# V rows of the expert mix in one transfer for four expert tiles

## What is computed

```
def block(hb):                                # hb: 128 tokens x 1024
    q = (hb @ wq).reshape(n, 8, 2, 128)
    s = einsum('thpk,hpnk->thpn', q, keys)
    ...                                       # top 16 of 128 x 128 key pairs per head
    eidx, gw = chosen experts (8 heads x 16), softmax of their scores
    a = einsum('thkd,td->thk', u_tab[eidx], hb)
    w = gelu(a) * gw
    return einsum('thk,thkd->td', w, v_tab[eidx])
```

## Time and profile before

| | |
|---|---|
| runs | 5314.53, 5320.29, 5320.93 us; median 5320.29 |
| profiled execution | span 5317.0 us; its total time beside the span is not given |
| VectorE busy | 3482.5 us, 65% |
| TensorE busy | 4329.9 us, 81% |
| second stage of the mixer, layer 0 | from 2088.7 to about 2956 us |
| second stage of the mixer, layer 1 | from 4664.5 to about 5282 us |
| V loads (line 1907) | 256 transfers of 512 KB |
| activation loads (line 1906) | 128 of 192 KB, 128 of 128 KB |
| gathers of V (line 1917) | 640 |
| gate loads (line 1905) | 8 of 3 MB, 8 of 2 MB |

### The profile page before, as it was taken

One profiled execution on the slowest core, in us unless ns is written; L12 is line 12 of the kernel. 1 busy time (PEld: TensorE's weight loads), 2 busy tenths in 40 slices (PEclk: granted clock), 3 DMA queues, 4 the chain that ended last, 5 costly groups with the idle time before them and its releaser, 6 DMA issues. The chain is left out here.

```text
span 5317.0 us, 58819 instructions
## 1 busy us (share of the span) xinstructions
PE 4329.9 (81%) x21260; PEld 3195.8 (60%) x21260; DVE 3482.5 (65%) x6809; ACT 1481.4 (28%) x2724; POOL 1522.0 (29%) x1488
## 2 busy tenths in 40 slices
PE   6976788889999994887888676677689998867886
PEld 5854786766666663444445434333468888756776
DVE  3146763249979786787788534899329968645665
ACT  2125322223445553000000224544223455500000
POOL 0000330004324454344444000355003334333441
PEclk8988898989999996899899878888889999988987
DMA  4211002139879999999999100111238989999996
GB/s 160 64 65 64 5 5 80 48 146 352 317 273 340 414 404 394 363 394 392 378 383 393 50 18 9 42 48 44 79 120 321 342 334 398 376 364 402 403 403 240
DMA packets 465036, 1252.92 MB, mean 236 GB/s; under 512 B 52055, under 2 KB 186957, under 8 KB 459117
## 3 DMA queue, kind: packets, MB, share of 16 engines
q0 software_dynamic: 184320, 671.17, 32.9%
q1 hardware_dynamic: 275984, 569.51, 29.0%
q10 hardware_dynamic: 4444, 8.48, 0.4%
HBM read 1146.24 MB, written 102.76 MB: 235 GB/s over the span
## 5 line engine op out<-in xcount | busy, mean ns | idle before, releaser
L1935 PE MATMUL banks<-acts_in,v_rows 128*128 128x384 f32 (+1 forms) x4096 | 1161.2, 446 | 304.5 <-DMA v_rows<-peer_v 173.3
L1558 PE MATMUL banks<-h_dense,u_t 128*128 128x384 f32 (+1 forms) x4096 | 1205.8, 438 | 0.0
L1935 PEld LDWEIGHTS banks<-acts_in,v_rows 128*128 128x128 f32 x4096 | 796.3, 196 | 669.1 <-DMA v_rows<-peer_v 194.4
L1532 POOL DMA_INDIRECT rows<-peer_u,expert x640 | 633.5, 990 | 1508.6 <-DVE weight L1835 816.2
L1558 PEld LDWEIGHTS banks<-h_dense,u_t 128*128 128x128 f32 x4096 | 750.7, 193 | 249.1 <-issue 4.4
L1835 DVE CUSTOM_DVE_ANT_0 rows<-rows,banks 128x1024 f32<-128x1024 f32 x640 | 764.9, 1211 | 197.7 <-DMA rows<-peer_u,expert 132.5
L1917 POOL DMA_INDIRECT v_fetched<-peer_v,expert x640 | 608.1, 950 | 862.1 <-DVE banks L1997 745.0
L1997 DVE SCALAR_TENSOR_TENSOR banks<-v_fetched,weight,banks 128x1024 f32<-128x1024 f32 x630 | 783.3, 1279 | 0.0
L1926 ACT COPY y_tok<-banks 128x1024 f32<-128x1024 f32 x5 | 5.1, 1012 | 1461.7 <-DVE banks L1997 1461.7
L1973 DVE TENSOR_TENSOR acts_in<-acts_in,gates 128x384 f32<-128x384 f32 (+1 forms) x256 | 124.6, 487 | 431.1 <-DMA acts_in<-activations 431.0
L1617 ACT COPY u_t<-banks 128x512 f32<-128x512 f32 x512 | 300.2, 587 | 300.8 <-PE banks L1549 298.3
(11 more groups left out here) (403 smaller groups left out, 6239.0 us busy)
## 6 DMA issues: line engine op xcount, KB each, us to landing
u_raw<-peer_u SPq DMA_DIRECT2D x256, 512.0 KB, 7.9
v_rows<-peer_v SPq DMA_DIRECT2D x256, 512.0 KB, 15.2
gate_table<-part SPq DMA_DIRECT2D x20, 2048.0 KB, 11.8
activations<-acts SPq DMA_DIRECT2D x128, 192.0 KB
gates<-gate_table SPq DMA_DIRECT2D x8, 3072.0 KB, 22.8
acts_in<-activations SPq DMA_DIRECT2D x128, 192.0 KB, 12.4
peer_wq_in<-peer_wq SPq DMA_DIRECT2D x16, 1024.0 KB, 5.4
ada_ring<-ada_w SPq DMA_DIRECT2D x32, 512.0 KB, 3.9
```

The costliest lines, as they stand in the source:

```text
L1532: pool.indirect_dma_start(out=ring[:, s % U_RING, :], out_offset=None, in_=rows_of_u, in_offset=bass.IndirectOffsetOnAxis(ap=expert[:, t, ...
L1558: last = nc.tensor.matmul(out, u_t[:, i % 2, k * P:(k + 1) * P], h[:, k], start=(k == 0), stop=(k == DK - 1))
L1935: return nc.tensor.matmul(y_at(m if RESIDENT else j // GROUP * DK + m), v[:, j % V_ROWS, m * P:(m + 1) * P], acts[:, j % V_ROWS], start=st ...
```

## The change

Instead of one load of 512 KB for each expert tile, the first tile of a group issues one load of 2 MB for the group's four tiles. The order of issue in a group becomes: gates where due, activations of tile 0, V of tiles 0 to 3, activations of tiles 1, 2 and 3. The semaphores of V are two instead of eight, one for each half of the ring, and TensorE's `ready(j)` waits for the half in which j lies.

```diff
@@ -1869,7 +1869,7 @@
-        v_loaded, acts_loaded = ([a.sem(f"{name}{r}") for r in range(V_ROWS)] for name in ("v_loaded", "acts_loaded"))
+        v_loaded, acts_loaded = ([a.sem(f"{name}{r}") for r in range(n)] for name, n in (("v_loaded", V_ROWS // GROUP), ("acts_loaded", V_ROWS)))
@@ -1904,7 +1904,9 @@
                 sp.dma_start(acts[:, j % V_ROWS], acts_d[j]).then_inc(acts_loaded[j % V_ROWS], 16)
-                sp.dma_start(v[:, j % V_ROWS:j % V_ROWS + 1], v_rows[:, j:j + 1, :]).then_inc(v_loaded[j % V_ROWS], 16)
+                if r == 0:
+                    sp.dma_start(v[:, j % V_ROWS:j % V_ROWS + GROUP], v_rows[:, j:j + GROUP, :])\
+                        .then_inc(v_loaded[i % (V_ROWS // GROUP)], 16)
                 if j == V_ROWS - 1:
                     sp.dma_start(g.x_t[:], x_d).then_inc(x_loaded, 16)
@@ -1928,7 +1930,7 @@
             def ready(j):
-                pe.wait_ge(v_loaded[j % V_ROWS], 16 * (j // V_ROWS + 1))
+                pe.wait_ge(v_loaded[j % V_ROWS // GROUP], 16 * (j // V_ROWS + 1))
                 pe.wait_ge(weighted, j + 1)
```

## The result

The changed kernel takes 5349.66 us (median of 4 runs, 5341.98 to 5354.22) against 5320.61 for the kernel before (4 runs). The ratio is 1.0054, 95% interval 1.0039 to 1.0068: slower by 29 us. That is on the side that was forecast and inside the range, and about twice the predicted 15 us. The profiled execution has a span of 5346.0 us against 5317.0, which is the same 29 us.

What follows compares the result with a forecast made beforehand. Layer 0 was taken as bound by VectorE's work plus activation waits, layer 1 by nearly full DMA and TensorE. Terms 63 - 38 - 6 - 2 - 2 gave +15 us, predicted 5335 us, range 5296 to 5366.

Steps and rivals of the forecast that it cites:

- the distance of 7.5 to 8 us: Sign in layer 0: a group's first and second multiplies that far apart, with a wait near 2.75 us.
- TensorE's group-wide semaphore: V's semaphore standing for a whole group: nothing in layer 0; in layer 1 counted in that layer's -2 us.
- The wait before the second multiply: Layer 0, mid-block: V delays the second activation tile, a new VectorE wait of 2.75 us in 23 groups, +63 us.
- What comes back at the gates: Layer 0: fewer gathers under way shorten each of seven gate waits by 5.5 us, -38 us.
- First multiplies: Layer 0, activation waits outside gates and startup: TensorE catches up, SP issues earlier, -6 us (0 to -12).
- The second multiply behind gates: Layer 0, behind a gate load: q0 has run dry, so the wait there is only 0.2 us.
- Issues: SP in each layer: 96 fewer issues of 0.43 us; SP mostly waits for TensorE anyway, so nothing.
- Layer 1: Lower DMA floor against TensorE needing all four V tiles behind gates: -2 us, bounds -10 and +8.
- TensorE's chain of 72.9 us: Layer 1, per block: 59.6 us of products plus a 13.3 us gap, which does not get shorter.
- the DMA's floor: Layer 1: larger packets save 12 us of DMA time, lowering the floor by 1.5 us a block.
- the DMA is the bound, bigger packets simply pay: Rival for the whole kernel: gate waits absorb the new wait, engine time saved gives -22, 5298 us; chance 0.22.
- The fixed cost per transfer: Rule of 2.0 us per DMA plus bytes, about 4936 us; rival of a fixed queue cost, 5301 us, chance 0.01.

Runs made afterwards that it cites:

- e1: The changed kernel with the 2 MB load of V behind the group's four activation tiles instead of behind the first; ratio to the kernel before 0.9989.
- e2: The kernel before with its four 512 KB loads of V moved up behind the group's first activation tile; ratio to the kernel before 1.0285.
- e6: The changed kernel with V in transfers of two tiles (1 MB, 8 KB to a partition) and four semaphores; ratio to the kernel before 0.9971.
- e4: The change made in layer 1 alone, layer 0 as in the kernel before; ratio to the kernel before 0.9971.
- e3: The kernel before with its four 512 KB loads of V moved down behind the group's four activation tiles; ratio to the kernel before 1.0000.
- e7: The kernel before with each gate load but the first issued behind the loads of the group before; ratio to the kernel before 1.0002.
- e9: The kernel before with each gate load cut in four, the quarters issued behind the loads of the four groups before; ratio to the kernel before 0.9944.

## Why the prediction was right

**Who waits, and for what.** That layer 0 is VectorE's fixed work plus its waits for activations held: waits +39.8 us, time +42 us, work unchanged. Of the signs that the prediction named, the distance of 7.5 to 8 us (8.0) and the 64 transfers came as said; the gate waits are 14.1 us and not 12, the waits in layer 0 222.8 and not near 200, and layer 1's block, 71.7 us, is just under its 72 to 75. That TensorE's group-wide semaphore costs layer 0 nothing held too: e1 has it and has no loss.

**The wait before the second multiply** was the main term, computed as 2.75 us and 63 us from a packet of 16 KB at the rate of x's packets and turns of one each. Measured: 2.87 us in the mean and 66.0 us, the single waits 2.0 to 4.7 us. e2 and e6 put two other numbers to the same rule, 7.1 and 0.4 us expected, 6.3 and 0.4 measured. The page counts 64 transfers of V of 2048 KB and 248336 packets in q1 in place of 275984. That is 27648 fewer: 24576 where four V packets of 4 KB became one of 16 KB, and 3072 more, which is 16 for each of the 192 transfers fewer.

**What comes back at the gates** is the term that failed: -38 forecast, -22 measured, 16 of the 23 us by which layer 0's +17 fell short of +39.8. Its mechanism was right. The gathers issued about a gate load (from 6 us before it to 1 us after) land fast in the changed kernel, here for the load at 2536.82:

```profile
DMA to landing us min/median/max: 5.2/5.3/5.6
```

Over the seven loads the medians are 5.1 to 7.0 us, so few gathers are backed up there any more, and the gate loads themselves land 2.9 us sooner in the median. The seven of layer 0, before and after:

```profile
DMA to landing us min/median/max: 21.3/22.9/23.8
...
DMA to landing us min/median/max: 17.3/20.0/21.0
```

Two steps of the size were off. I took the 13.5 us of one block as the state of all: over the seven loads before the change the medians are 10.0 to 13.7 us, 12.1 in the mean against 5.9 after, so (12.1 - 5.9) / 1.7 = 3.7 gathers or 4.8 us were to be had on the average, not 6.2. And in the first 4 us after the issue of a gate load its own packets hardly come, while q0 runs on. The queues in those 4 us, before (from 2507.47) and after (from 2536.82):

```profile
q0 software_dynamic: 430, 1.57, 98.3%
q1 hardware_dynamic: 36, 0.06, 4.1%
```

```profile
q0 software_dynamic: 302, 1.08, 78.2%
q1 hardware_dynamic: 89, 0.18, 12.1%
```

Before the change 128 gather packets more went out of the way before the gates came, 8 for each engine or 1.3 us (over the seven loads q0 moved 439 packets in the mean before and 306 after). On this account they never cost the gate load anything. 4.8 - 1.3 is 3.5 us; measured are 22.0 / 7 = 3.1. The sum fits; no run tests this second step by itself.

**First multiplies** gave 3.7 of the 6 us. **The second multiply behind gates** has the 0.2 us that I computed and then left out of the sum, but 1.8 us behind the first of the loads, 3.2 us together.

**Issues** were put at nothing because eight take under 4 us. That holds in mid-block and not behind gates: in layer 0 before the change one issue of 7.1 to 9.3 us follows each of the seven gate loads, and several of the next ones take about 1.8 us and not 0.43. From SyncE's timeline, behind a gate load and in the next group:

```profile
2405.81 8.25 SPq L1906 DMA_DIRECT2D acts_in<-activations  x1
2414.10 2.46 SPq L1907 DMA_DIRECT2D v_rows<-peer_v  x1
...
2445.33 0.43 SPq L1907 DMA_DIRECT2D v_rows<-peer_v  x1
```

The changed kernel has such issues too, so nothing was gained or lost by it that these runs show.

**Layer 1** was forecast at -2 and gave -14. The step that failed is TensorE's chain of 72.9 us, which I said would not get shorter. TensorE's busy time in the six blocks is 58.6 us a block before and 58.2 after; I had put 59.6, 16 times the 3.72 us of one tile's row. And the one gap of 13.3 us behind the gates was not all its waiting. TensorE's waits for V (its weight loads) in one block, in us, times and longest, before and after:

```profile
PEld banks L1935 <- DMA v_rows<-peer_v: 17.1, 5, 13.7
...
PEld banks L1937 <- DMA v_rows<-peer_v: 14.6, 2, 14.3
```

The gap behind the gates grew by 0.6 us, as the prediction had feared, but the small waits for V in the middle of the block went. Over layer 1 TensorE's waits for V fell from 131.2 us to 121.4 and its busy time from 472.0 to 467.9, which together are the 14 us:

```profile
L1937 PE MATMUL banks<-acts_in,v_rows 128*128 128x256 f32 x2048 | 467.9, 393 | 121.4 <-DMA v_rows<-peer_v 121.4
```

What stays is the DMA's floor, which I had at -1.5 us a block and which is measured as -1.4 (73.1 to 71.7). The startup and the first block gave the rest, about 6 us. So the rival "the DMA is the bound, bigger packets simply pay" is true of layer 1, and e4 has it alone. Windows of layer 1 from 4800 to 5200 us bear it out: 402 to 403 GB/s in every kernel with 4 KB packets there (before, e2, e3, e7, e9), 406 in e6 with 8 KB, 407 to 408 in every one with 16 KB. It is false of layer 0, where the changed kernel leaves the DMA at 369 GB/s.

**The fixed cost per transfer.** With 192 transfers fewer the time rose, and the 4936 us of the single rule weighed in the prediction are 414 us away. The fit that it rests on stands in the Trainium skill, "DMA: Bandwidth & Descriptors", not in the section on bandwidth but under "Anatomy of one DMA — SWDGE (gpsimd) path", for transfers that GpSimd issues; V's loads are issued by SyncE and stand in a queue that is kept full, and no run here shows that cost.

**Clock.** The six blocks of layer 0 have a mean granted clock of 0.93 of 2.4 GHz after and 0.92 before, so these rows show no loss of clock by the new short waits, as assumed.

The two misses, 16 us at the gates and 12 us in layer 1, have opposite signs. Layer 0 by itself was forecast at +17 and came out at +42; that the total was only 14 us off is in part luck.

## What to carry to other kernels

When small transfers are merged, the order of the queue changes with them: a small load that stands behind the merged one is late by the time that the merged one takes, and here that decided more than the number of transfers. Compute where the next consumer's tile lands against when it asks, and put the small tiles that an engine needs soon ahead of the large one that it needs late. The same holds for a rare large load in front of frequent small ones: with the gate loads cut in pieces and spread over the groups, the gate waits in layer 0 fell from 121.0 to 5.3 us and the layer took 34 us less, where issuing them earlier in one piece did nothing; in layer 1, with a full DMA, spreading brought nothing either. And look which resource is full in each stage: one edit gained in the stage with a full DMA and lost in the one that lives by a wait.

## What the runs showed of the hardware that was not expected

- The waits behind V fit two queues that take turns by packets, whatever their size (4, 8 and 16 KB tried), so that a queue's share of the engines follows the size of its packets. Turns of a few packets each would give the same sums, since a V transfer and a gather are both eight packets for each engine; these runs do not tell the two apart. The same 2 MB held up the tile behind it for 3.4 us less in packets of 16 KB than of 4 KB (2.9 against 6.3 us of wait, 2.75 and 7.1 computed).
- Larger packets for 29% of layer 1's bytes (67.1 MB of V in 234.9 MB) raised the rate of a full DMA from 402 to 407 GB/s, whatever the order of the loads.
- An issue on SyncE can take twenty times as long when a large load of small pieces stands in the queue: behind each 3 MB gate load in pieces of 2 KB one took 7.1 to 9.3 us, against 0.43 in mid-block. With the gate loads cut in four (e9) the issues in layer 0 stayed at 0.32 to 0.44 us from 2178 us on, but for one of 0.69; in its layer 1, with a full DMA, some still took up to 5.3 us. What limits the issue is not shown.
- The kernel before differed by 16 us in its median from one set of runs to the next (5316.2 to 5332.0, on another chip), as much as e4 or e6 gained, while ratios taken within a set have intervals of 0.1 to 0.3% to either side.
